# Order of the first loads, the division by the root mean square, and two square buffers, in the first stage of a two-block sequence model

## The reference

```python
def rms_norm(x, g):
    var = jnp.mean(x * x, axis=-1, keepdims=True)
    return x * lax.rsqrt(var + EPS) * g
sh_l, sc_l, gt_l = jnp.split(jax.nn.silu(c) @ ada_w[0] + ada_b[0], 3, axis=-1)
h_lat = rms_norm(x, norm_g[0]) * (1.0 + sc_l[:, None]) + sh_l[:, None]
...
h_ctx = rms_norm(ctx, norm_g[0]) * (1.0 + sc_c) + sh_c
# the first mixer then projects h_lat and h_ctx, head by head
```

## Time and profile before

| what | value |
|---|---|
| median of 3 runs | 2747.86 us (2746.51 to 2750.76) |
| profiled execution, own time | 2748.82 us |
| its span, first to last instruction | 2747.2 us |
| TensorE busy | 2564.4 us, 93% of the span |
| VectorE busy | 1625.9 us, 59% |
| ScalarE busy | 1027.7 us, 37% |
| GpSimd busy | 13.1 us |

### The profile page before, as it was taken

One profiled execution on the slowest core, in us unless ns is written; L12 is line 12 of the kernel. 1 busy time (PEld: TensorE's weight loads), 2 busy tenths in 40 slices (PEclk: granted clock), 3 DMA queues, 4 the chain that ended last, 5 costly groups with the idle time before them and its releaser, 6 DMA issues.

```text
span 2747.2 us, 40135 instructions
## 1 busy us (share of the span) xinstructions
PE 2564.4 (93%) x14516; PEld 2191.1 (80%) x14516; DVE 1625.9 (59%) x2388; ACT 1027.7 (37%) x1349; POOL 13.1 (0%) x28
## 2 busy tenths in 40 slices
PE   6999999999999988999899999989999889999996
PEld 2788888888888775888688999988888757788885
DVE  5567777777777754333345443457999855534445
ACT  3334443444344323333234322235455533542222
POOL 0000000000000000000000000000000000000000
PEclk9999999999999998999899999999999999999998
DMA  5212211121112222222122222222222212222232
GB/s 219 69 62 76 70 61 61 62 83 61 61 53 89 79 85 69 69 69 69 45 94 74 91 87 92 92 92 85 89 87 91 85 54 88 89 99 92 92 99 84
DMA packets 59817, 224.34 MB, mean 82 GB/s; under 512 B 6496, under 2 KB 6496, under 8 KB 59136
## 3 DMA queue, kind: packets, MB, share of 16 engines
q1 hardware_dynamic: 56544, 207.94, 22.3%
q0 software_dynamic: 3232, 15.86, 1.5%
HBM read 221.68 MB, written 2.10 MB: 81 GB/s over the span
## 4 chain that ended last, share of the span: by engine, by line
PE 79%; DVE 9%; ACT 5%; issue 5%; DMA 1%; DVEq 0%; ACTq 0%; SPq 0%; POOL 0%
PE ps L409 71%; PE ps L568 3%; ACT w_hi L812 2%; PE ps L590 1%; DVE K L1469 1%; PE ps L466 1%; DVE w_lo L1265 1%; DVE cv L1826 1%; ACT K_now L932 1%; PE ps L581 1%; ACT L910 1%; DVE f_tree L1461 1%; DMA ada_raw<-in_ada_weights_dram 1%; PE ps L609 1%; DVE n_tmp L1826 0%
## 5 line engine op out<-in xcount | busy, mean ns | idle before, releaser
L1265 DVE TENSOR_TENSOR w_lo<-w_raw,w_hi 128x1024 fp32r<-128x1024 f32 x360 | 440.2, 1223 | 618.2 <-ACT w_hi L812 616.4
L812 ACT ACTIVATE w_hi<-w_raw 128x1024 fp32r<-128x1024 f32 x360 | 381.2, 1059 | 973.3 <-PE ps L409 939.5
L409 PE MATMUL ps<-n_hi,w_hi 128*128 128x512 f32 (+1 forms) x992 | 323.8, 358 | 29.7 <-DVE w_lo L1265 15.4
L409 PE MATMUL ps<-n_lo,w_hi 128*128 128x512 f32 (+1 forms) x992 | 320.2, 355 | 0.0
L409 PE MATMUL ps<-n_hi,w_lo 128*128 128x512 f32 (+1 forms) x992 | 319.8, 354 | 0.0
L409 PE MATMUL ps<-h_hi,w_hi 128*128 128x512 f32 x640 | 273.0, 427 | 9.2 <-DVE h_lo L1292 4.6
L409 PE MATMUL ps<-h_hi,w_lo 128*128 128x512 f32 x640 | 255.0, 398 | 0.0
L409 PE MATMUL ps<-h_lo,w_hi 128*128 128x512 f32 x640 | 254.8, 398 | 0.0
L409 PEld LDWEIGHTS ps<-n_hi,w_hi 128*128 128x128 f32 x992 | 175.4, 191 | 65.9 <-issue 20.2
L409 PEld LDWEIGHTS ps<-n_lo,w_hi 128*128 128x128 f32 x992 | 176.0, 190 | 26.7 <-issue 0.2
L409 PEld LDWEIGHTS ps<-n_hi,w_lo 128*128 128x128 f32 x992 | 175.8, 190 | 26.6
(11 more groups left out here) (327 smaller groups left out, 5012.9 us busy)
## 6 DMA issues: line engine op xcount, KB each, us to landing
w_raw<-in_weights_dram SPq DMA_DIRECT2D x376, 512.0 KB, 3.3
ada_raw<-in_ada_weights_dram SPq DMA_DIRECT2D x4, 2048.0 KB, 25.2
gate_raw<-in_gate_weights_dram POOLq DMA_DIRECT2D x16, 512.0 KB, 4.8
x<-in_x_dram SPq DMA_DIRECT2D x1, 2048.0 KB, 9.3
x<-in_x_dram POOLq DMA_DIRECT2D x1, 2048.0 KB, 11.1
out_dram<-fin POOLq DMA_DIRECT2D x1, 2048.0 KB, 6.5
xc<-in_ctx_dram POOLq DMA_DIRECT2D x1, 1024.0 KB, 10.7
F_raw<-in_seq_dft_dram POOLq DMA_DIRECT2D x1, 1024.0 KB, 5.5
```

The source lines that it names most:

```text
L409: last = nc.tensor.matmul(o, w, xp, start=start and n == 0, stop=stop and n == 2)
L812: run(w_hi[:, s], w_raw[:, s], ACT.Copy).then_inc(hi_ready[s], 1)
L1265: tt(w_lo[:, s], w_raw[:, s], w_hi[:, s].bitcast(F32), ALU.subtract).then_inc(lo_ready[s], 1)
```

## The change

The edits, all in the first stage:

- SyncE issues modulation load 0 ahead of x, and ctx after load 1. GpSimd no longer loads ctx; it waits for ctx before the identity, and for modulation load 3 before masks and gate block.
- TensorE makes the mean of x within load 1 (ahead of its last two tiles) and the mean of ctx after load 1, in PSUM bank 5.
- ScalarE squares into two buffers (`st_tmp`, `st_tmpc`) and waits only for the add before the last one. It, and no longer VectorE, copies the four parts of the modulation row. Both roots come before the weight cuts.
- VectorE multiplies the tiles of x, and after the weight cuts those of ctx, by the inverse root in place, before the modulation is known (`over_root`). When it is, ScalarE makes the upper part directly from the tile with scale and shift (`first_hi`), and VectorE makes the whole value with one `ts` and subtracts the upper part with one `tt` (`first_lo`).
- `norm_apply` loses its argument `inverted`; its other uses stay.

```diff
@@ -290,7 +290,7 @@
         consts_set = sem("consts_set")
         small = {e: sem(f"small_{e}") for e in ("act", "dve")}
         own_s = {e: sem(f"own_{e}") for e in ("act", "dve")}
-        ada_done, ada_copied = sem("ada_done"), sem("ada_copied")
+        ada_done, ada_copied, ada_scaled = sem("ada_done"), sem("ada_copied"), sem("ada_scaled")
         acc_free = sem("acc_free")
         pe_scan, act_scan, dve_scan = sem("pe_scan"), sem("act_scan"), sem("dve_scan")
         PE_SCAN, ACT_SCAN, DVE_SCAN = 18, 7, 11
@@ -366,9 +366,12 @@
         @block.sync
         def _(sp):
             sp.dma_start(vec[:], vec_in).then_inc(vec_in_s, 16)
-            sp.dma_start(x0[:], x_in).then_inc(x_in_s, 16)
             for n, (dst, a, b_) in enumerate(ADA_LOADS):
                 sp.dma_start(dst, ada_in[a:b_].rearrange("b p n -> p b n")).then_inc(ada_loaded[n], 16)
+                if n == 0:
+                    sp.dma_start(x0[:], x_in).then_inc(x_in_s, 16)
+                elif n == 1:
+                    sp.dma_start(xc[:], ctx_in).then_inc(xc_in_s, 16)
             with sp.Fori(0, nblocks // 2) as i:
                 for s in range(2):
 
@@ -379,9 +382,10 @@
 
         @block.gpsimd
         def _(pool):
-            pool.dma_start(xc[:], ctx_in).then_inc(xc_in_s, 16)
+            pool.wait_ge(xc_in_s, 16)
+            pool.dma_start(ident[:], ident_in).then_inc(ident_in_s, 16)
+            pool.wait_ge(ada_loaded[3], 16)
             pool.dma_start(masks[:], mask_in).then_inc(const_in_s, 16)
-            pool.dma_start(ident[:], ident_in).then_inc(ident_in_s, 16)
             with pool.Fori(0, HEADS) as i:
                 pool.wait_ge(gate_used, i + 1)
                 pool.dma_start(gate_raw[:], gate_in[ds(i, 1)].rearrange("a p n -> p (a n)")
@@ -434,7 +438,7 @@
             def bank2(b):
                 return [ps[:, b, 0:HALF], ps[:, b + 1, 0:HALF]]
 
-            def mean(N, n, src, added=None):
+            def mean(N, n, src, added=None, bank=6):
 
                 if added:
                     pe.wait_ge(added["add"], KD + 1)
@@ -445,7 +449,7 @@
                         last = nc.tensor.matmul(ps[:, 6 + q, 0:HALF], ones_d[:], src[:, q * HALF:(q + 1) * HALF],
                                                 start=True, stop=True)
                 else:
-                    last = nc.tensor.matmul(ps[:, 6, 0:n], ones_d[:], src[:, 0:n], start=True, stop=True)
+                    last = nc.tensor.matmul(ps[:, bank, 0:n], ones_d[:], src[:, 0:n], start=True, stop=True)
                 last.then_inc(N["mean"], 1)
 
             def tile_cols(t):
@@ -459,21 +463,22 @@
             pe.wait_ge(consts_set, 1)
             pe.wait_ge(small["act"], 1)
             for n, (raw_, a, b_) in enumerate(ADA_LOADS):
-                if n == 3:
-                    mean(N0, T, st_sum[:, 0])
                 pe.wait_ge(ada_loaded[n], 16)
                 for k in range(KD):
+                    if n == 1 and k == KD - 2:
+                        mean(N0, T, st_sum[:, 0])
                     last = nc.tensor.matmul(ps[0:2, n], csil[:, k], raw_[:, :, k * P:(k + 1) * P],
                                             start=k == 0, stop=k == KD - 1)
                 last.then_inc(ada_part, 1)
+                if n == 1:
+                    mean(N0C, TC, st_sum[:, 1], bank=5)
             pe.wait_ge(ident_in_s, 16)
-            pe.wait_ge(ada_copied, 1)
+            pe.wait_ge(ada_copied, 4)
             for m_ in range(16):
                 last = nc.tensor.transpose(ps[:, 7, 2 * m_:2 * m_ + 2], ada_row[:, m_ // 4, tile_cols(m_ % 4)],
                                            ident[0:2, 0:2])
             last.then_inc(ada_done, 1)
-            pe.wait_ge(N0["root"], 1)
-            mean(N0C, TC, st_sum[:, 1])
+            pe.wait_ge(N0C["root"], 1)
 
 
             def tile(t):
@@ -834,9 +839,9 @@
             def squares(R, src, sq):
 
                 for k in range(KD):
-                    if k:
-                        act.wait_ge(R["add"], k)
-                    run(sq, src(k), ACT.Square).then_inc(R["sq"], 1)
+                    if k > 1:
+                        act.wait_ge(R["add"], k - 1)
+                    run(sq(k), src(k), ACT.Square).then_inc(R["sq"], 1)
 
             def square_one(R, m_, src, sq, credit):
 
@@ -857,17 +862,34 @@
             act.wait_ge(consts_set, 3)
             run(rgc[:, 1], rgc[:, 0], ACT.Exp, scale=-1.0).then_inc(small["act"], 1)
             act.wait_ge(x_in_s, 16)
-            squares(R0, lambda k: x0[:, k], st_sq[:])
+            squares(R0, lambda k: x0[:, k], lambda k: st_tmp[:, k % 2])
+
+            def copy_ada(n):
+
+                act.wait_ge(ada_part, n + 1)
+                run(ada_row[:, n], ps[0:2, n], ACT.Copy).then_inc(ada_copied, 1)
+
+            copy_ada(0)
             act.wait_ge(xc_in_s, 16)
-            act.wait_ge(R0["add"], KD)
-            squares(R0C, lambda k: xc[:, k], st_sq[:, 0:TC])
-            act.wait_ge(R0C["add"], KD)
+            squares(R0C, lambda k: xc[:, k], lambda k: st_tmpc[:, k % 2])
             root(N0, ps[:, 6], st_sq[:])
+            root(N0C, ps[:, 5, 0:TC], st_tmpc[:, 2])
+            copy_ada(1)
             cut(0)
             cut(1)
-            norm_hi(N0, lambda k: h_hi[:, k], lambda k: st_tmp[:, k % 2], lambda k: ada0[:, k, 0:1])
-            root(N0C, ps[:, 6, 0:TC], st_tmpc[:, 2])
-            norm_hi(N0C, lambda k: hc_hi[:, k], lambda k: st_tmpc[:, k % 2], lambda k: ada0[:, k, 1:2])
+            copy_ada(2)
+            copy_ada(3)
+
+            def first_hi(N, hi, src, n):
+
+                for k in range(KD):
+                    act.wait_ge(N["tmp"], k + 1)
+                    run(hi(k), src(k), ACT.Identity, bias=ada0[:, k, n:n + 1], scale=scale[:, n, k:k + 1]
+                        ).then_inc(N["hi"], 1)
+
+            act.wait_ge(ada_scaled, 1)
+            first_hi(N0, lambda k: h_hi[:, k], lambda k: x0[:, k], 0)
+            first_hi(N0C, lambda k: hc_hi[:, k], lambda k: xc[:, k], 1)
 
 
             def act_head(i, j, f):
@@ -1273,15 +1295,14 @@
                     dve.wait_ge(R["sq"], k + 1)
                     if k:
                         dve.wait_ge(R["add"], k)
-                        tt(acc, acc, sq, ALU.add).then_inc(R["add"], 1)
+                        tt(acc, acc, sq(k), ALU.add).then_inc(R["add"], 1)
                     else:
-                        v.tensor_copy(acc, sq).then_inc(R["add"], 1)
-
-            def norm_apply(N, src, gain, shift, tmp, rt_, hi, lo, inverted=False):
-
-                if not inverted:
-                    dve.wait_ge(N["root"], 1)
-                    own.link(v.reciprocal(rt_, rt_))
+                        v.tensor_copy(acc, sq(k)).then_inc(R["add"], 1)
+
+            def norm_apply(N, src, gain, shift, tmp, rt_, hi, lo):
+
+                dve.wait_ge(N["root"], 1)
+                own.link(v.reciprocal(rt_, rt_))
                 for k in range(KD + 1):
                     if k < KD:
                         if k > 1:
@@ -1354,21 +1375,25 @@
             own.link(stt(p_, p_, 2.0, rgc[:, 5], ALU.mult, ALU.add))
             ts(rgc[:, 6], p_, -8.0, None, ALU.mult)
             own.mark(ts(rgc[:, 7], p_, 8.0, None, ALU.mult))
-            sum_squares(R0, KD, st_sum[:, 0], st_sq[:])
+            sum_squares(R0, KD, st_sum[:, 0], lambda k: st_tmp[:, k % 2])
             dve.wait_ge(R0["add"], KD)
             dve.sem_inc(N0["sum"], 1)
-            sum_squares(R0C, KD, st_sum[:, 1, 0:TC], st_sq[:, 0:TC])
+            sum_squares(R0C, KD, st_sum[:, 1, 0:TC], lambda k: st_tmpc[:, k % 2])
             dve.wait_ge(R0C["add"], KD)
             dve.sem_inc(N0C["sum"], 1)
-            for n in range(3):
-                dve.wait_ge(ada_part, n + 1)
-                v.tensor_copy(ada_row[:, n], ps[0:2, n])
-            dve.wait_ge(N0["root"], 1)
-            own.mark(v.reciprocal(st_sq[:], st_sq[:]))
-            dve.wait_ge(ada_part, 4)
-            v.tensor_copy(ada_row[:, 3], ps[0:2, 3]).then_inc(ada_copied, 1)
+
+            def over_root(N, x, rt_):
+
+
+                dve.wait_ge(N["root"], 1)
+                own.link(v.reciprocal(rt_, rt_))
+                for k in range(KD):
+                    tt(x[:, k], x[:, k], rt_, ALU.mult).then_inc(N["tmp"], 1)
+
+            over_root(N0, x0, st_sq[:])
             cut(0)
             cut(1)
+            over_root(N0C, xc, st_tmpc[:, 2])
 
             dve.wait_ge(ada_done, 1)
             own.link(tt(ada0[:, 0:16], ps[:, 7, 0:32].rearrange("p (m n) -> p m n", n=2),
@@ -1378,10 +1403,22 @@
                 own.mark(stt(scale[:, n], ada0[:, 8:16, n:n + 1].rearrange("p k n -> p (k n)"), 1.0, g0,
                              ALU.add, ALU.mult))
             own.wait()
-            norm_apply(N0, lambda k: x0[:, k], lambda k: scale[:, 0, k:k + 1], lambda k: ada0[:, k, 0:1],
-                       lambda k: st_tmp[:, k % 2], st_sq[:], lambda k: h_hi[:, k], lambda k: h_lo[:, k], inverted=True)
```

(18 more changed lines are left out.)

## The result

The changed kernel takes 2733.68 us (median of 5 runs, 2732.18 to 2734.57) against 2747.86 before (5 runs, 2746.43 to 2751.38): a ratio of 0.9945 with a 95% interval of 0.9931 to 0.9960, so 14.2 us less, 0.5%. The forecast was 2733.5. The profiled execution took 2732.18, span 2730.5.

What follows compares the result with a forecast made beforehand. TensorE has 79% of the chain, so starting it earlier should pay: third block 12.7 us earlier plus 1.66 of low clock, sum 14.4; 2748.82 - 14.4 = 2734.4, median 0.96 lower, 2733.5; range 2729 to 2741.

Steps and rivals of the forecast that it cites:

- Loads: Start of the kernel: reordered loads land modulation load 0 at 8.6 us, x at 13.3, load 1 at 19.4.
- TensorE idles for 2.4 us: Modulation: TensorE waits between blocks 0 and 1, then block 1 pays 1.66 us of low clock; passes end at 43.5.
- The two buffers: Sums of squares on ScalarE and VectorE: a second buffer is worth nothing on the path, covered by 6 us.
- Copy and transposes: After the modulation passes: row copy on ScalarE 0.6 us, transposes 1.3 later, ending at 45.4.
- VectorE in the gap: Before the modulation is known: VectorE's inversions, products and cuts end at 45.6 us, level with the transposes; thin cover.
- The tiles: After the bias: new operation 0.47 us, subtraction 0.69, pace 1.11 per tile of x; last lower part at 55.1.
- Third block: Head 0's third weight block starts at 64.3 us, not 77.05, without a hole; its 1.66 us of low clock go too.
- (a): Rival on the tiles: single-source operation costs as much as now, products and load 1 late; time 2738 us; chance 0.12.
- (b): Rival: TensorE keeps its clock over the 2.4 us hole and transfers land early; time 2731 us; chance 0.12.
- (c): Rival: lower clock lasts through all of head 0's blocks one and two, losing 10.3 us; time 2744; chance 0.04.
- (d): Rival: masks, issued late on GpSimd's software queue, hold up VectorE's cut for block three; slower than before; chance 0.02.
- (e): Rival: loads not reordered in effect, ada 0 and x mixed; +0.7 us, 2734; folded into the forecast, together 0.67.

Runs made afterwards that it cites:

- c: Changed kernel with one buffer for the squares instead of two; median 2737.99 us, ratio to the kernel before 0.9944 to 0.9971.
- e: Kernel before with two buffers for the squares and nothing else; median 2749.43 us, ratio to the kernel before 1.0003.
- g: Changed kernel with four buffers for the whole values of x and three for ctx instead of two; median 2733.61 us.
- d: Changed kernel with the old tile arithmetic, inverse roots still early but multiplied in the tile after the modulation; median 2738.12 us.
- f: Changed kernel with the four copies of the modulation row back on VectorE; median 2736.53 us.
- b: Kernel before with the new order of loads alone; median 2741.59 us.
- h: g plus, in head 0, TensorE's upper-part passes of weight blocks 0 and 1 ahead of the lower-part ones; median 2731.26 us.

## Why the prediction was right, and where its steps were not

*Loads: right in order, load 0 too early.* Load 0 at 9.86 (8.6 taken), load 1 at 19.79 (19.4), squares of x from 14.66 (13.3). The transfers came in the order of issue, each 1.1 to 1.8 us later than its byte sum. The byte sums took the 300 GB/s of the first 8.2 us from the earlier trace rows; in the changed kernel, where SyncE's queue alone loads then, the same window has 257 GB/s. That is 0.35 MB less, 0.9 us at 0.40 MB per us. Of the case that ada 0 and x mix, the trace shows nothing: TensorE has load 0 almost 5 us ahead of x. The Trainium skill's rule of unordered completion (DMA: Bandwidth & Descriptors, section on queues, rings and completion order) had no effect that can be seen here.

*TensorE: close sum from two wrong terms.* The step "TensorE idles for 2.4 us" and the cold block of 1.66 us were both wrong. Load 0 landed 1.3 us later and its own block took 9.42 us instead of 8.4, so the hole was 0.51 us, and block 1 ran at full speed (twelve passes in 5.31). That it did is not owed to this short hole alone: in the seven profiles with the new order the hole was 0.24 to 1.51 us and block 1 equally fast behind it. What a hole of 2.4 us would have cost here, no run shows. With load 1 0.4 us late and 1.66 not paid the end came at 42.43 instead of 43.5. In all of these profiles block 1 starts when load 1 has landed, however long block 0 took, so the start of the chain is load 1 and not load 0.

*The two buffers: wrong.* "The ctx sum (from 21.1 ...) ends at 25 ... So the two buffers are worth nothing on the path" let ctx start when it has landed. With one buffer x is summed only until 25.6, ctx queues behind it on both engines, and its sum ends at 32.4. Runs c and e show what stands in its place: nothing under the old order, about 6 us under the new. The total was right all the same because the change has both edits, so that no term of the sum rests on this price; for the mechanism that is luck.

*Copy and transposes: right.* Copy 0.60 (0.6), transposes end at 44.31 (45.4, all of the difference from the step before).

*VectorE in the gap: right, size too high.* It ended at 43.16 (45.6), since the products follow each other by 0.61 and 0.34 instead of the full durations 0.69 and 0.43, and the inversion of the root began 1.3 earlier.

*The tiles: sizes off.* The new operation takes 0.545 (0.47 on the line between 128 and 1536 columns), the subtraction 0.684 (0.69). The pace is 1.18 against 1.11; g shows that 0.12 of it is the wait for a free buffer, a term that I did not have. The last lower part came at 54.3 (55.1).

*Third block: right.* 63.66 (64.3), no hole, clock kept; in d, where ScalarE has to wait for VectorE's tiles again, a hole of 0.67 us is back.

*Sum.* The third block came 13.39 us earlier (12.7), and its full clock gave another 1.6 (1.66): 15.0 at the anchor against 14.4, and 14.2 by medians. It was kept through the rest of the program (15.03 at 936 us). That the median is within 0.2 us of the forecast is luck: the terms on the path were off by up to 1.7 us and made up for each other, and the medians of the kernel before alone differ by 1.4.

*The rivals.* (a) took 0.75 us for the new operation, the forecast 0.47; it takes 0.545, and the late products did not occur, though f shows how close they were. (b) came true in one half, no cold block, though not because TensorE kept its clock over a long hole. (c): the clock was low from 46.7 to 52 (0.50, the row below), then full, and the first block did not pay for it, since VectorE's lower parts set its end: the chain of waits comes from VectorE until 53.72. Its sum was also too high: with a low pass of 0.43 us and a full one of 0.235 a second block of 8.4 us grows by 7.0, not by 8.4. (d): the masks were issued at 33.35 and landed 3.9 us later, long before they were wanted. That VectorE's two-port operations could hold such a load up (the Trainium skill, SBUF — State Buffer, section on who interferes with whom) no run here shows: the load was over before the first new tile (37.25 and 44.96). (e), the mixed landing of ada 0 and x, did not occur, as said above.

```profile
46.70:52.00 5.30, 5.29 (x13) 4.09 (x14) 5.15 (x10) 5.30 (x9) 0.00 (x0) 0.50 0.01 3
```

## What to carry to other kernels

When a step is moved to the front, ask of every chain behind it when it is now due and on which engines it queues; a buffer that buys nothing in one order (e) can be worth some six microseconds in another (c, by the anchor; 4.3 by the medians). In a stage that waits for two inputs, load first what feeds the longest chain, and put the work that needs only the other one (here the division by the root) into the wait. Two operations that alternate over two buffers may still wait for each other; count the buffers by what has been issued, not by what has ended.

## What the runs showed of the hardware that I had not expected

The same hole of 1.81 us before the third block was followed by a low clock in the kernel before (0.52 for 3.45 us, 120 passes in 24.27) and in e (0.52 for 3.51 us), and by a full clock in b (22.71). Behind 3.87 us in c it was low. Between the passes over the modulation weights, holes of 0.24 to 1.51 us were never followed by slower passes, nor was the 0.67 in d. But ahead of head 0, where only the 16 small transposes (in before and b also the mean of ctx) stand between two waits, 1.56 us (h), 2.41 (changed kernel), 3.19 (d) and 3.23 (before) were all followed by a granted clock of 0.50. So the length of a hole alone does not tell whether the clock falls, and a cost for a hole of such a length is an either-or, not a number.

The first passes of the program ran slowly while the page's granted clock said 1.00. In a window of the changed kernel:

```profile
9.86:14.20 4.34, 4.34 (x6) 0.71 (x7) 0.24 (x2) 0.00 (x0) 0.00 (x0) 1.00 0.96 410
```

Six passes in 4.34 us are 0.72 each, against 0.43 later; in all the first block took 9.42 us, against 22.16 - 2 x 6.95 = 8.3 when it started at 19.70. The start 10 us earlier does not set this by itself: the seven profiles with the new order start the block between 9.47 and 10.24, and it took from 8.40 us (g) to 9.70 (f). What sets the length was not tried. It cost nothing, since load 1 landed later than the block ended in all seven.
